# The sample's attention and the prompt's input projection in one stage of a decoder step

## The reference

```python
def _qkv(x, g, w):                       # w is (1024, 3072), six parts of 512 columns
    proj = _rmsnorm(x, g) @ w
    qa, ka, va, qb, kb, vb = jnp.split(proj, cuts, axis=-1)
...
    # stick-breaking attention of 8 heads of 64: over a paged cache for the sample
    z = einsum('bqhd,bkhd->bhqk', q, k) * hd ** -0.5 + sb_bias
    log_1m = where(mask, log_sigmoid(-z), 0)
    a = where(mask, exp(log_sigmoid(z) + cumsum(log_1m, reverse) - log_1m), 0);  o = a @ v
...
    # dilated window attention of 8 heads: windows (128,1), (512,4), (2048,16),
    # combined by softmax denominators, with a bias by distance from a table of 32 buckets
...
    mixed = concat([_rmsnorm(o_a, g_sb), _rmsnorm(o_b, g_dil)]) @ w_out
    x = x + mixed
    x = x + square(relu(_rmsnorm(x, g_mlp) @ w_up)) @ w_down        # 4096 hidden
    y = _rmsnorm(x, g_final)
```

## Time and profile before

| | us |
|---|---|
| median of 3 runs (lowest, highest) | 2215.3 (2209.49, 2215.92) |
| the profiled execution | 2211.82 |
| its span in the trace | 2210.0 |
| PE busy, share of the span | 1801.2, 81% |
| DVE busy | 936.0, 42% |
| ACT busy | 556.4, 25% |
| POOL busy | 531.8, 24% |
| mean DMA rate over the span | 169 GB/s |

### The profile page before, as it was taken

How to read it: one execution, slowest core, us unless ns; L and a number is a source line. 1 busy time by engine, 2 the same in 40 slices (tenths; PEclk the granted TensorE clock), 3 DMA queues, 4 the chain that set the end, 5 groups by cost and what they waited for, 6 DMA issues and landing times. The chain is left out here.

```text
span 2210.0 us, 37863 instructions
## 1 busy us (share of the span) xinstructions
PE 1801.2 (81%) x16830; PEld 1590.4 (72%) x16834; DVE 936.0 (42%) x857; ACT 556.4 (25%) x908; POOL 531.8 (24%) x377
## 2 busy tenths in 40 slices
PE   4999997487887825665666579699999999999997
PEld 4999995265655613333333469699999999999997
DVE  5310112477776639766765274722212212122223
ACT  4100101466667402221322310321121212111122
POOL 3111200000000025665665410321112112211210
PEclk7999996699999957878888789799999999999999
DMA  6222317711200059999999820433433333343332
GB/s 220 79 89 78 107 44 287 252 39 39 77 11 10 26 159 414 419 422 422 421 420 408 326 83 1 152 114 133 153 114 131 134 132 114 128 156 114 114 131 92
DMA packets 118370, 373.89 MB, mean 169 GB/s; under 512 B 18121, under 2 KB 59593, under 8 KB 106185
## 3 DMA queue, kind: packets, MB, share of 16 engines
q0 software_dynamic: 40192, 251.94, 29.0%
q1 hardware_dynamic: 74712, 117.92, 15.4%
q10 hardware_dynamic: 3360, 2.47, 0.4%
HBM read 336.58 MB, written 102.57 MB: 199 GB/s over the span
## 5 line engine op out<-in xcount | busy, mean ns | idle before, releaser
L404 POOL TENSOR_TENSOR mlp_w_lo<-mlp_raw,mlp_w_hi 128x2048 fp32r<-128x2048 f32 x30 | 138.1, 4603 | 587.9 <-ACT mlp_w_hi L450 587.9
L1285 PE MATMUL sa_s<-sa_kT,sa_qd 128*32 128x256 f32 x1344 | 129.0, 550 | 155.6 <-DVE sa_kT L1549 97.1
L1285 PEld LDWEIGHTS sa_s<-sa_kT,sa_qd 128*32 128x32 f32 x1344 | 52.5, 146 | 213.3 <-DVE sa_kT L1549 104.7
L563 DVE TENSOR_TENSOR xT<-xT,mlp_acc 128x1088 f32<-128x1088 f32 x64 | 82.4, 1287 | 280.0 <-PE mlp_acc L145 280.0
L145 PE MATMUL mlp_acc<-n_hi,mlp_w_hi 128*128 128x272 f32 x1024 | 172.1, 290 | 20.7 <-POOL mlp_w_lo L121 16.3
L1549 DVE STREAM_TRANSPOSE sa_kT<-sa_k_in 128x2048 f32<-128x2048 f32 x64 | 147.1, 2306 | 78.5 <-DMA sa_k_in<-in_cache_sb_k,sa_k_rows 75.5
L145 PE MATMUL mlp_acc<-mlp_h_hi,mlp_w_hi 128*128 128x272 f32 x1024 | 170.7, 288 | 3.9 <-DVE mlp_h_lo L559 3.9
L145 PE MATMUL mlp_acc<-n_hi,mlp_w_lo 128*128 128x272 f32 x1024 | 171.2, 289 | 0.0
L145 PE MATMUL mlp_acc<-n_lo,mlp_w_hi 128*128 128x272 f32 x1024 | 171.2, 289 | 0.0
L145 PE MATMUL mlp_acc<-mlp_h_lo,mlp_w_hi 128*128 128x272 f32 x1024 | 169.9, 288 | 0.0
L145 PE MATMUL mlp_acc<-mlp_h_hi,mlp_w_lo 128*128 128x272 f32 x1024 | 169.9, 288 | 0.0
(11 more groups left out here) (178 smaller groups left out, 3168.9 us busy)
## 6 DMA issues: line engine op xcount, KB each, us to landing
out<-in_cache_win_k POOLq DMA_DIRECT2D x16, 2040.0 KB, 8.8
out<-in_cache_win_v POOLq DMA_DIRECT2D x16, 2040.0 KB, 8.8
mlp_raw<-in_w_up SPq DMA_DIRECT2D x16, 1024.0 KB, 11.8
mlp_raw<-in_w_down SPq DMA_DIRECT2D x16, 1024.0 KB, 11.7
qkvT<-qkv_out SPq DMA_DIRECT2D x24, 544.0 KB, 2.7
qkv_raw<-in_w_in SPq DMA_DIRECT2D x12, 1024.0 KB, 5.4
na_rows_in<-qkvT SPq DMA_DIRECT2D x16, 544.0 KB, 7.0
out<-na_nat POOLq DMA_DIRECT2D x4, 2048.0 KB, 10.8
```

Source lines behind the costliest of these rows:

```text
L404: pool.tensor_tensor(out=ring.lo[:, n % 2, :], in0=ring.raw[:, n % 2, :], in1=ring.hi[:, n % 2, :].bitcast(F32), op=ALU.subtract).then_inc ...
L563: dve.tensor_tensor(in_banks(xT[:, c, :]), in_banks(xT[:, c, :]), acc[:, c % 2, :, 0:BW], ALU.add).then_inc(added, 1)
L1285: last_one = pe.matmul(out[h * 32:(h + 1) * 32, :], qd[:, k, x, :], keys[:, x, :], start=(b == 0), stop=(b == 1 and stop))
```

## The change

The prompt's projection is taken out of the dense stage and put in the same stage as the sample's attention; the sample's own projection, the bias tables and the row numbers of the gathers move to a new first stage.

- Before: gains, tokens, dense (1088 columns), natural, prompt, sample, out, MLP, store. After: `first_stage`, `projection_and_sample_stage`, `natural_stage`, `prompt_stage`, out, MLP, store.
- `first_stage` turns the tokens (the sample's first), makes `hi` and `lo` of the prompt's 1024 columns and the root of their mean squares (on PE from the squares, 16 products with ones), projects the 64 sample rows with the tokens as stationary operand and plain float32 weights as moving one (12 steps of 1.05 MB of weights, 192 products), stores their rows, mirrors the queries in time on POOL, and makes and lays out the window bias, `f` = 0 and then 1.
- The weights come from the host in a layout of 24 contiguous chunks of 128 x 1024, and are read twice: by the first stage as float32 and by the joint stage, which splits them.
- In the joint stage the projection is 48 banks (24 chunks of 128 features, two halves of 512 columns), each 24 products of 512 columns. Four banks are in step 0, then one is in each step up to 44. `bank(z, 0)` stands between the scores and the values of a step, `bank(z, 1)` behind the values.
- Rings: keys 3 halves, turned keys 2 halves (`KT`), values 5 quarters (one sequence of a unit each), weights 4 units. Scores are released by halves. Values follow the scores by 4 steps; in the window units two are turned in one step.
- Queries and new keys come as natural rows of 8 tokens by DMA and are transposed by DVE, in place of PE transposes of padded tiles. `prod` is no longer a buffer of its own; the running products are made in place in `stay`.
- `natural_stage` has no sample rows and no bias table, and three PSUM slots in place of two.

```diff
-def load_tokens(nc, cx, x_prompt, x_sample, ident, xT):
-def gains_stage(nc, cx, gains, ident_in, ident, ones):
+def first_stage(...):
+    NX, NW = 4, 3
+    pairs = [(4, 3), (1, 0), (5, 2)]
+    steps = [(j, u) for j in range(3) for u in range(W // P)]
...
+                load_tile(0)
+                sp.dma_start(ident[:, :], ident_in).then_inc(ident_loaded, 16)
+                for t in range(1, 3):
+                    load_tile(t)
+                sp.dma_start(rb[:, :], rel_bias).then_inc(table_loaded, 16)
...
+                for i in range(len(steps)):
+                    load_weights(i)
+                    if i == 5:
...
+                        sp.dma_start(xT_kept.rearrange("(c p) t -> p c t", p=P), xT[:, :, :]).then_inc(kept, 16)
...
+                def project(i):
+                    j, u = steps[i]
+                    pe.wait_ge(w_loaded[i % NW], 32 * (i // NW) + 32)
+                    for k in range(KC):
+                        for x in range(2):
...
+                            last = pe.matmul(acc[x * NS:(x + 1) * NS, j, cols], xs[:, k, back * NS:(back + 1) * NS],
+                                             w[:, i % NW, x, k * P:(k + 1) * P], start=(k == 0), stop=(k == KC - 1))
...
+                for i in range(4):
+                    project(i)
+                for c in range(KC):
+                    pe.wait_ge(squared, c + 1)
+                    for b in range(SEQ // QB):
+                        last = pe.matmul(turned[:, 0, b * QB:(b + 1) * QB], ones[:, :], square[:, c % 2, b * QB:(b + 1) * QB], ...)
+                    last.then_inc(added, 1)
+                for i in range(4, len(steps)):
+                    project(i)
...
+                act.wait_ge(bias_stored, 16)
+                load_bias(0)
+                for c in range(KC):
...
+                    act.activation(hi[:, c, :], xT[:, c, 0:SEQ], ACT.Copy, scale=gains[0][0][:, c:c + 1]).then_inc(hi_done, 1)
+                    if c >= 2:
+                        act.wait_ge(added, c - 1)
+                    act.activation(square[:, c % 2, :], xT[:, c, 0:SEQ], ACT.Square).then_inc(squared, 1)
...
+                act.wait_ge(bias_done, 2 * ND + G)
+                load_bias(1)
...
-def sample_stage(...):
+def projection_and_sample_stage(...):
-    LAG = 6
-    KS, VS, WS = 4, 3, 7
+    KS, KT, VS, WS = 3, 2, 5, 4
+    BANKS = SEQ // QB
+    NZ = CHUNKS * BANKS
+    AHEAD = 4
+    def turn_step(n):
+        m = n % NU
+        return n // NU * NU + (6, 6, 7, 7, 8, 9)[m] if m <= ND else n + 3
+    STEPS = turn_step(N - 1) + 3
+    for z in range(NZ):
+        banks[max(0, z - AHEAD + 1)].append(z)
...
+                for s in range(STEPS):                      # SP
+                    for z in banks[s]:
+                        if z % BANKS == 0 and 2 <= z // BANKS + 1 < CHUNKS:
+                            load_weights(z // BANKS + 1)    # waits lo_done
+                        store_bank(z)                       # waits acc_out, z + 1
...
+                for s in range(STEPS):                      # POOL
+                    for x in range(2 * s + KS + 2, 2 * s + KS + 4):
+                        if x < 2 * N:
+                            load_keys(x)                    # waits kT_done, x - KS + 1
+                    for z in banks[s]:
+                        if z % BANKS == BANKS - 1 and 2 <= z // BANKS + 1 < CHUNKS:
+                            low(z // BANKS + 1)
+                    for n in turned_in(s - 1):
+                        for y in range(G * n + VS, G * n + VS + G):
+                            if y < G * N:
+                                load_values(y)              # waits valued, y - VS + 1
...
+                def bank(z, half):
+                    if half == 0:
+                        pe.wait_ge(lo_done, c + 1)
+                        if z >= 3:
+                            pe.wait_ge(acc_out, z - 2)
+                    for k in range(half * KC // 2, (half + 1) * KC // 2):
+                        for part, (w, x) in enumerate(((w_hi, hi), (w_hi, lo), (w_lo, hi))):
+                            last_one = pe.matmul(acc[:, z % 3, :], w[:, k, :], x[:, k, cols], ...)
...
+                for s in range(STEPS):                      # PE
+                    for n in turned_in(s - 2):
+                        if last(n):
+                            place(n)
+                    for z in banks[s][:-1]:
+                        bank(z, 0)
+                        bank(z, 1)
+                    if s < N:
+                        score(s)
+                    for z in banks[s][-1:]:
+                        bank(z, 0)
+                    for n in turned_in(s - 1):
+                        if first(n):
+                            values_new(n)
+                        values(n)
+                    for z in banks[s][-1:]:
+                        bank(z, 1)
+                    for n in turned_in(s):
+                        if first(n):
+                            turn_new(n)
+                        turn(n)
...
+                evict(0)                                    # DVE
+                turn_keys(0)
+                for z in banks[0][1:-1]:
+                    evict(z)
+                for s in range(STEPS):
+                    if s + 1 < N:
+                        turn_keys(s + 1)                    # waits scored, x - KT + 1
...
+                    for z in banks[s][-1:]:
+                        evict(z)
```

More of the change, by code:

```diff
@@ L60 @@
 BW = T // NB
-def load_tokens(nc, cx, x_prompt, x_sample, ident, xT):
-    half = KC // 2
-    tiles = [(t * P, P) for t in range(QT)] + [(SEQ, NS)]
-    with ExitStack() as st:
[L68 to L71, removed]
+QB = 512
@@ new lines, in _ @@
+                pe.wait_ge(mirrored, 2)
+                pe.wait_ge(left_out, len(tiles))
+                pe.wait_ge(right_out, len(tiles))
+                for c in range(KC):
+                    pe.matmul(turned[:, 1, 0:1], xq[:, c, :], ones[:, 0:1], start=(c == 0), stop=(c == KC - 1))
+                for x in range(2):
+                    for c in range(KC):
+                        last = pe.matmul(turned[x * NS:(x + 1) * NS, 1, 1:2], xq[:, c, 0:NS], ones[:, 0:1], start=(c == 0),
+                                         stop=(c == KC - 1))
@@ new lines, in _ @@
+                last.then_inc(summed_s, 1)
+                for i in range(4):
+                    project(i)
+                for c in range(KC):
+                    pe.wait_ge(squared, c + 1)
+                    for b in range(SEQ // QB):
+                        last = pe.matmul(turned[:, 0, b * QB:(b + 1) * QB], ones[:, :], square[:, c % 2, b * QB:(b + 1) * QB],
+                                         start=(c == 0), stop=(c == KC - 1))
+                    last.then_inc(added, 1)
+                for i in range(4, len(steps)):
+                    project(i)
@@ L581, in store_stage @@
         turned = st.enter_context(nc.psum_tensor("y_turned", [P, SLOTS, D_MODEL], F32))
-        gain_in, turn_done, squared, rooted, inverted, scaled, stored = cx.old
+        gain_in, turn_done, squared, rooted, inverted, scaled, stored = (cx.again() for _ in range(7))
         with nc.Block() as block:
@@ L1253, in _ @@
[L1253 to L1265 removed]
+                pool.memset(nat[:, :], 0.0).then_inc(nat_cleared, 1)
@@ L1494, in copy_out @@
                        .then_inc(stored, 16)
-                act.wait_ge(tables_ready, 6)
-                for s in range(N + LAG + 2):
-                    n, no = s - LAG, s - LAG - 2
-                    if 0 <= n < N and first(n):
-                        new_out(n)
+                split(0)
+                split(1)
+                act.wait_ge(tables_ready, 3)
+                for s in range(STEPS):
+                    for z in banks[s]:
+                        if z % BANKS == BANKS - 1 and 2 <= z // BANKS + 1 < CHUNKS:
+                            split(z // BANKS + 1)
+                    for n in turned_in(s - 2):
+                        if last(n):
+                            copy_out(n)
+                    for n in turned_in(s):
+                        if first(n) and kind(n) == SB:
+                            new_out(n)
                     if s < N and kind(s) == SB:
@@ L1505, in _ @@
                         gate(s)
-                    if 0 <= no < N and last(no):
-                        copy_out(no)
-                    if 0 <= n < N:
+                    for n in turned_in(s):
+                        if first(n) and kind(n) == DIL:
+                            new_out(n)
                         weights_out(n)
```

686 lines of the change are left out of this document (391 added, 295 removed).

## The result

The changed kernel takes 2153.4 us (median of 4 runs, 2145.39 to 2154.51) against 2215.6: ratio 0.9715, 95% interval 0.9684 to 0.9746. It is faster, but 114 us slower than the 2039 that I forecast and outside the range of 1980 to 2125.

What follows compares the result with a forecast made beforehand. PE bound the old dense stage and DMA the sample's, one behind the other; joined, DMA would still end last. First stage 94 + joint 562 + natural 50 + prompt 369.5 + later stages 961.6 + 1.8 outside = 2039 us, range 1980 to 2125.

Steps and rivals of the forecast that it cites:

- steps 1 to 6: Start of the joint stage: steps 1 to 5 load keys only, PE-bound, 5 x 7.5 = 37 us; step 6 takes 8.5.
- steps 7 to 10: Group 1's window units in the joint stage: three steps with paired values at 20 us, one at 12, 72 in all.
- steps 21 to 24: Joint stage, after the 20 ordinary steps' term and before steps 25 to 27: 46 us for these four steps.
- Part 2: Waits that the smaller rings add in the joint stage; steps with paired values 20 us, whole stage 562 (500 to 700).
- Step 9: Joint stage, group 1's window step with one unit's values instead of a pair: 12 us.
- The ordinary step: Joint stage: DMA ends last at 11.2 us, over PE's 9.8; with little slack for value gathers, 11.7 us was taken.
- A bank: Projection on PE in the joint stage: 24 products at 225 ns, 5.4 us; all banks 259 us (246 to 271).
- First stage: Replaces 345.2 us before the joint stage: tokens, 19.2 MB of loads at 421 GB/s, closing waits; 94 us (78 to 125).
- natural: Natural stage without its sample rows stays bound by DMA: 50 us instead of 55.0, bounds 45 and 55.
- the prompt: The prompt's attention stage, unchanged at 369.5 us, expected within 5 us.
- the clock: Rival: PE at half clock sets joint-stage steps at 18.5 us, whole 2315; clock or unseen stall above 2190: 0.05.
- shallow rings: Rival: every joint-stage step waits for a landing, 13.5 to 14.5 us; stage 650 to 700, whole 2127 to 2177; 0.24.

Runs made afterwards that it cites:

- the control: Changed kernel with the low part of the prompt's x cut to one chunk, high part used instead, value ring still five quarters: 2153.1 us, 0.9727.
- best_whole: Changed kernel with whole bank ahead of values (second half cut up between two-unit turns), next group's rows prepared apart, first-stage stores last: 2107.9 us, 0.9500.

## Why the prediction was wrong, by its steps

My terms of the joint stage against the changed kernel and the run with eight quarters (step starts from the timeline):

| | forecast | changed | eight quarters |
|---|---|---|---|
| start to score 1 | 34 | 38.4 | 39.7 |
| steps 1 to 6 | 45.5 | 59.4 | 65.2 |
| steps 7 to 10 | 72 | 100.6 | 72.3 |
| steps 11 to 20 | 117 | 121.6 | 113.3 |
| steps 21 to 24 | 46 | 60.4 | 56.1 |
| steps 25 to 27 | 24.5 | 28.0 | 32.4 |
| steps 28 to 31 | 72 | 91.8 | 67.0 |
| the rest | 151 | 156.7 | 139.1 |
| sum | 562 | 656.9 | 585.1 |

**The step that failed** is in Part 2: "PE alone would need 12.3, DMA 16.2; with issue and landing I take 20". Five quarters were named there, but priced as if the gathers of a pair could run ahead. They measured 31.6, 24.6 and 26.1 us. Step 7 is a sum and not the longer of PE and DMA: 9.1 us to the end of the fifth quarter, 12.9 of waiting for the sixth, 3.9 for the last three, 5.8 for the half bank and the turns. The wait was in the prediction, the length of the chain in front of it (key transposes, two key gathers, then the value gathers) was not. With eight quarters the pair steps took 15.2, 23.2, 15.5 and 15.7, 15.8, 16.2 us. That those steps then sum to 72.3 and 67.0, near my 72, is partly luck: the pair steps came out at 17 on average, below 20, and the 12 of step 9 was 18.4. The whole stage gets 72 us back from those three quarters (76 against the control): the ring's size is shown as the main cause of the missing 95. It is not the only way at them: with five quarters and values first on POOL, steps 7 to 10 fell by 16 us.

**Step 9** is long for another reason. In every kernel with the whole projection and the turns behind the bank it takes 18 to 20 us, twelve quarters included. PE in the changed kernel, behind the bank that ends at 272.6:

```profile
273.55 0.71 PE L1580 MATMUL sa_w<-ident,sa_take 128*128 128x128 f32 x4 [0.56 <-ACT sa_wn L1703]
276.64 1.10 PE L1580 MATMUL sa_w<-ident,sa_take 128*128 128x128 f32 x4 [2.38 <-ACT sa_wtsT L1711]
279.52 1.89 PE L1620 MATMUL sa_m<-sa_tok,sa_o_own 128*128 128x32 f32 x8 [1.78 <-DVE sa_o_own L1855]
```

The turn of new weights, two units' turns and the placing stand in a row with ACT and DVE, 8.7 us, and I had counted the turns as PE work alone. Cutting the bank up between them gave 17.7 (`best_whole`), hardly anything.

**The ordinary step** was sound: 11.7 forecast, 12.2 measured in steps 11 to 20, 11.3 with eight quarters. It mostly alternates, 10.2 without POOL's low part and up to 16.3 with it; I had priced the third gather's delay, but not the low clock behind it.

**A bank** takes 0.233 us a product, in my bounds of 214 to 235 but not my 225: 1152 x 0.008 = 9 us of PE work. **Steps 1 to 6** cost 14 us more: step 1 took 15.2, not 7.5. In it PE waited 5.1 us for a low part that POOL began at 152.2, behind five value gathers, two key gathers and 1.7 us of waiting for ACT, then ran half a bank at the low clock, and DVE waited 9.0 us for keys gathered behind that low part. The larger rings put more value gathers in front and made it longer (16.6 and 22.1 us with eight and twelve); no run took this cause away by itself. **Steps 21 to 24** took 60.4 for 46; with `prep(3)` done apart 56.4, so it was 4 us of the 14, and the rest stays open.

**First stage**, 109.0 for 94. Its windows:

```profile
50.00:60.00 10.00, 8.35 (x41) 5.49 (x42) 0.00 (x0) 1.78 (x2) 4.56 (x14) 0.64 1.02 418
60.00:70.00 10.00, 9.99 (x22) 3.61 (x21) 6.42 (x5) 9.98 (x11) 0.00 (x0) 1.00 0.67 275
70.00:80.00 10.00, 6.64 (x99) 5.41 (x97) 6.72 (x2) 2.57 (x4) 0.00 (x0) 1.00 0.55 128
80.00:90.00 10.00, 0.00 (x0) 0.00 (x0) 0.00 (x0) 0.00 (x0) 0.00 (x0) 0.55 0.94 250
```

I divided its bytes by 421 GB/s. They moved at 275 and 128 while, or just after, the 16.0 us of squares' sums (55.3 to 71.2) kept PE from freeing weight tiles, and then at 250 with the DMA engines at 0.94 busy. The two stretches lie one behind the other. The second bias load and the weights overlap in the last; that this makes the 250 was argued, not tested.

**Right** were natural (48.7 for 50), the prompt (369.1 for 369.5), the rest, and the clock: 0.90 over the stage, so that rival is out. The time falls in the rival "shallow rings" (2127 to 2177, given 0.24). Its place was wrong, though: it let every step wait 13.5 to 14.5 us, and it was the pair steps. It named the Trainium skill's 358 GB/s (SBUF — State Buffer, "Summary: rules for kernel authors"), whose estimate of 640 came near the measured 657. The trace does not bear out the reason, a rate that cannot be passed: with twelve quarters, loads and stores together moved at 411 GB/s in the window 507 to 609 (351 over that run's whole joint stage, with its slow start):

```profile
507.00:609.00 102.00, 93.47 (x1423) 76.20 (x1416) 65.36 (x58) 22.79 (x56) 65.41 (x60) 0.94 1.02 411
```

## What to carry to other kernels

When a ring shrinks, price it by the largest burst of its consumer, not by the mean: a ring that holds a whole burst lets the loads run ahead, and a ring short of it puts issue, queue and landing in line with the work. Bursts of eight quarters took rings of 5, 8 and 12 to 2153, 2074 and 2069 us: what lies beyond the burst gave little. Work that is to cover a landing belongs in front of the wait; behind it, it covers nothing, and here it then ran at the clock that the waits left. Where both the engine and the DMA are partly idle in the same stretch, look for the buffer between them before counting bytes or products.

## What was not expected of the hardware

VectorE's product of the gates, 0.69 us alone, took 3.00 us when POOL took a low part beside it. Timelines of DVE (steps 13 and 14) and POOL:

```profile
338.59 0.69 DVE L1848 TENSOR_TENSOR sa_take<-sa_take,sa_stay 128x512 f32<-128x512 f32 x1
...
349.11 3.00 DVE L1848 TENSOR_TENSOR sa_take<-sa_take,sa_stay 128x512 f32<-128x512 f32 x1
...
349.18 2.36 POOL L1433 TENSOR_TENSOR sa_wl<-sa_wr,sa_wh 128x1024 fp32r<-128x1024 f32 x1
```

3.00 is about 0.69 + 2.36, as if the two ran one behind the other. The Trainium skill (SBUF — State Buffer, "SBUF: two separate sides") says that VectorE with two inputs from SBUF and a GpSimd operation that reads SBUF lock each other out for the whole instruction; the trace agrees. It also stands at 205.35, just ahead of step 7 and the late key transposes (3.02 us), and I had not priced it.

The clock fell behind three short waits of 0.68, 1.46 and 0.64 us with 0.63 us of products between them; before, it stayed up behind a single one of 2.23 us.
